# One decoder layer on one Trainium2 core: memory scores kept in PSUM, and transposed outputs taken in one operation

## The chip, the cores and the metric

The kernel runs on one core of one Trainium2 chip. The metric is the device time of one execution in microseconds (us), as the median of several executions. TensorE (PE) multiplies matrices, VectorE (DVE) works elementwise and reduces, ScalarE (ACT) applies functions, GpSimd (POOL) and SyncE (SP) do side work and issue transfers. PSUM is the memory that PE writes to; here it is the tensor `ps`, eight banks of 128 partitions by 512 fp32 words. SBUF is the other on-chip memory.

## The reference

The layer has three groups of heads on one input projection, an output projection, and a mixture of 32 experts (top 4). The change touches only the attention of two of the groups:

```python
s = jnp.einsum('bnqhgd,bnkhd->bnhgqk', qb, kk).astype(jnp.float32) * scale   # sliding window, 6 heads
s = jnp.where(mask[None, :, None, None], s, -jnp.inf)
p = jax.nn.softmax(jnp.concatenate([s, sink], axis=-1), axis=-1)[..., :-1]
...
s = jnp.einsum('bshd,bmhd->bhsm', q, km).astype(jnp.float32) * (HEAD_DIM ** -0.5)   # memory, 4 heads
p = jax.nn.softmax(s, axis=-1)
o = jnp.einsum('bhsm,bmhd->bshd', p.astype(vm.dtype), vm)
```

The sequence has 1024 positions, so 8 blocks of 128; a block of window attention sees 256 keys (its own and the previous 128), and so does a block of memory attention (256 memory tokens). Each group's output is then RMS-normalised with its own gain and goes into the output projection.

## The kernel before

The kernel has one program per engine, and semaphores order them. The stages in time are: norms and the input projection with the recurrent branch; the attention; the output projection with the router; and a loop over the passes of the experts, which takes most of the time.

The attention runs over 16 items, `items`: for each of the 8 blocks first "swa" (sliding window, 6 heads), then "mem" (memory, 4 heads). Item j goes through these steps, each of which is a small function called in an order written out by hand:

- PE `scores(j)` (L1022): one product of 128 queries with 256 keys per head, into banks 0 to 3 of `ps`, which rotate: a swa item takes four banks (its last two heads alone in one each), a mem item two. `scb` counts banks; a bank is written again four banks later, after a wait on `sc_out`.
- DVE `softmax_in(j)`: for swa, three operations (L1521) that scale, add the mask and write to `scores_sb`; for mem, two operations (L1524) that only scale. Then one maximum over all heads (L1527), and a small operation that negates it into `nmx` (L1530, L1535; for swa L1533 too).
- ACT `exps(j, half)` (L684): one exponential per head over 256 keys, `scores_sb` to `scores_sb`, with `nmx` as bias; each also gives the row's sum.
- PE `transpose_probs(j)` (L1038): two heads at a time into bank 4 or 5, from where ACT `take_probs` (L697, bank 4) and DVE `softmax_out` (L1549, bank 5) copy them.
- PE `values(j)` (L1055) into bank 6; DVE `normalise(j)` (L1559) to `o_sb`; ACT `take_o(j)` (L706) squares it for the norm.
- PE `transpose_o(j)` (L1065) into bank 7; DVE `take_y(j)` (L1569): one operation per pair of heads (three for swa, two for mem) that multiplies by a gain column and writes `uT`, counted by `yt_out`.

PE's order for item j is `transpose_probs(j)`, `scores(j + 2)`, `values(j)`, `transpose_o(j - 1)`. DVE's is `normalise(j - 1)`, `softmax_out(j)`, `take_y(j - 2)`, `softmax_in(j + 2)`. ACT's is `exps(j + 1, 0)`, `take_probs(j)`, `exps(j + 1, 1)`, `take_o(j - 1)`, where half 0 holds the first half of the heads. Before this loop DVE does `softmax_in(0)`, `softmax_in(1)` and three products `uT` by gate (L1578), on which POOL's work for the recurrent branch (L494, L496, L498) waits. After it PE sums that branch's squares (L1082) and, once all of `yt_out` has come, starts the output projection `project` (L1102).

Of the kernel before, what the change touches and what calls it, by code (L numbers as in the profile page):

```python
# [22 lines left out]
ALU = mybir.AluOpType  # L23
ACT = mybir.ActivationFunctionType
AX_X = mybir.AxisListType.X

P = 128
# [5 lines left out]
DH = 64  # L33
# [38 lines left out]
def hymba_layer(nc, x, mem, g_mix, w_in, conv_w, conv_b, lru_wa, lru_ba, lru_wx, lru_bx, lru_lambda,  # L72
# [3 lines left out]
    with ExitStack() as ctx:  # L76
# [43 lines left out]
        uT = sb_early("uT", [P, NCT, S])  # L120
# [6 lines left out]
        band = ring[:, 11264:11776].rearrange("p (i k) -> p i k", i=2)  # L127
# [4 lines left out]
        scores_sb = ring[:, 0:4608].rearrange("p (b h k) -> p b h k", b=3, h=NQ)  # L132
# [27 lines left out]
        def col(i, n=1):  # L160
            return vecs[:, i:i + n]
# [6 lines left out]
        nmx, row_sums = ([st[:, base + 8 * i:base + 8 * (i + 1)] for i in range(3)] for base in (0, 24))  # L168
# [25 lines left out]
        with ExitStack() as between:  # L194
# [21 lines left out]
        ps = ctx.enter_context(nc.psum_tensor("ps", [P, 8, HALF], F32))  # L216
# [20 lines left out]
        in_done, in_out = sem("in_done"), sem("in_out")  # L237
# [5 lines left out]
        sc_done, sc_out, nmx_ready, exp_done, sink_in, sink_exp = map(  # L243
            sem, "sc_done sc_out nmx_ready exp_done sink_in sink_exp".split())
        pt_done, pt_act, pt_dve, pv_done, o_ready, o_ss, yt_done, yt_out = map(
            sem, "pt_done pt_act pt_dve pv_done o_ready o_ss yt_done yt_out".split())
# [53 lines left out]

        items = [(kind, b) for b in range(NT) for kind in ("swa", "mem")]

        def heads(kind):
            return NQ if kind == "swa" else NM

        def score_banks(kind):
            return [(0, 2), (1, 3), (4,), (5,)] if kind == "swa" else [(0, 2), (1, 3)]

        scb, hc, ytc = [0], [0], [0]
        for kind, _ in items:  # L310
            scb.append(scb[-1] + len(score_banks(kind)))
            hc.append(hc[-1] + heads(kind))
            ytc.append(ytc[-1] + heads(kind) // 2)
        ptac = [0]
        for kind, _ in items:
            ptac.append(ptac[-1] + (heads(kind) // 2 + 1) // 2)
# [265 lines left out]
        def _(act_e):  # L582
# [25 lines left out]
            for u in range(4):  # L608
                act_e.wait_ge(mkv_done, u + 1)
                dst = km[:, u, :] if u < 2 else vm[:, u - 2, :]  # L610
# [65 lines left out]
            def exps(j, half):  # L676
                kind, b = items[j]
                nh = heads(kind)
                if half == 0:
                    act_e.wait_ge(nmx_ready, j + 1)  # L680
                    if j >= 3:
                        act_e.wait_ge(o_ready, j - 2)
                for h in range(half * (nh // 2), (half + 1) * (nh // 2)):
                    act_e.activation(scores_sb[:, j % 3, h, :], scores_sb[:, j % 3, h, :], ACT.Exp,  # L684
                                     bias=nmx[j % 3][:, h:h + 1],
                                     accum_out=row_sums[j % 3][:, h:h + 1]).then_inc(exp_done, 1)
                if kind == "swa" and half:
                    act_e.wait_ge(sink_in, b + 1)
                    act_e.activation(sinkx[b % 2], sinkx[b % 2], ACT.Exp).then_inc(sink_exp, 1)
# [184 lines left out]
        def _(pe):  # L874
# [15 lines left out]
            for k in range(0, KD, 2):  # L890
                b = bank_of_transposes()
# [109 lines left out]
            def scores(j):  # L1001
                kind, b = items[j]
                lo = P if kind == "swa" and b == 0 else 0
                banks = score_banks(kind)
                for first in range(0, len(banks), 2):
                    for k in (first, first + 1):
                        u = scb[j] + k
                        if u >= 4:
                            pe.wait_ge(sc_out, u - 3)
                        else:  # L1010
                            pe.wait_ge(in_out, 21 + u)
                    for n in range(len(banks[first])):
                        for k in (first, first + 1):
                            h = banks[k][n]
                            r = slice(h % 2 * DH, (h % 2 + 1) * DH)
                            if kind == "swa":
                                qs = uT[r, Q + h // 2, b * P:(b + 1) * P]
                                keys = (uT[r, K, :] if h // 3 == h % 2 else k_other[r, :])[:, (b - 1) * P + lo:(b + 1) * P]
                            else:
                                qs = uT[r, QM + h // 2, b * P:(b + 1) * P]  # L1020
                                keys = km[r, h // 2, :]
                            m = pe.matmul(ps[:, (scb[j] + k) % 4, n * 256 + lo:n * 256 + 256], qs, keys, start=True, stop=True)  # L1022
                            if n == len(banks[k]) - 1:
                                m.then_inc(sc_done, 1)
# [361 lines left out]
        def _(dve):  # L1386
            chain = [0]

            def link(ins):

                chain[0] += 1
                ins.then_inc(dve_step, 1)
                dve.wait_ge(dve_step, chain[0])
# [10 lines left out]
            for n, (a, b) in enumerate(((0, 2), (2, 6), (6, 10))):  # L1404
# [19 lines left out]
                else:  # L1424
                    h = n - 1
                    for k in range(KD):
                        u = 4 + 8 * h + k
# [19 lines left out]
            for c in range(LT):  # L1447
                u, xc = uT[:, LRU + c, :], lru_s[:, 0, :]
# [8 lines left out]
                for back in (1, 2, 3):  # L1457
                    m = dve.scalar_tensor_tensor(out=xc[:, back:S], in0=u[:, 0:S - back], scalar=col(C_CONVW + 3 * (3 - back) + c),
                                                 in1=xc[:, back:S], op0=ALU.mult, op1=ALU.add)
# [4 lines left out]
                t, a, w = lru_s[:, 3, :], lru_s[:, 4, :], lru_s[:, 5, :]  # L1464
# [17 lines left out]
            for u, (h, n) in enumerate(norm_units):  # L1482
                t, w, g = normt[n]
# [3 lines left out]
                                         op0=ALU.mult, op1=ALU.mult).then_inc(normed, 1)  # L1487


            scale = DH ** -0.5  # L1490
            dve.wait_ge(rt_in, 16 * NRT)
            dve.wait_ge(pool_const, NPOOLC)
            link(dve.tensor_scalar(st[:, 88:94], sinkb[:, :], -1.0, None, ALU.mult))
# [1 line left out]
            def softmax_in(j):  # L1495
                kind, b = items[j]
                nh = heads(kind)
                sc = scores_sb[:, j % 3, 0:nh, :]
                banks = score_banks(kind)
                for k, hs in enumerate(banks[:3]):  # L1500
                    n = 2
                    dve.wait_ge(sc_done, scb[j] + (k + 1 if k < 2 else 4))
                    if j == 0 and k == 0:
                        dve.wait_ge(in_done, 24)
                    if j >= 3 and k == 0:
                        dve.wait_ge(pt_done, ytc[j - 2])
                    bank = (scb[j] + k) % 4
                    if k < 2:
                        src = ps[:, bank, :].rearrange("p (h k) -> p h k", h=n)
                        dst = scores_sb[:, j % 3, k:k + 3:2, :]  # L1510
                    else:
                        src = ps[:, bank:bank + 2, 0:256]
                        dst = scores_sb[:, j % 3, 4:6, :]
                    if kind == "swa":
                        if b == 0:

                            dve.tensor_copy(dst[:, :, 0:P], band[:, 1:2, 0:P].to_broadcast([P, n, P]))
                            src, dst, mk = src[:, :, P:2 * P], dst[:, :, P:2 * P], band[:, 1:2, P:2 * P].to_broadcast([P, n, P])
                        else:
                            mk = band[:, 0:1, :].to_broadcast([P, n, 2 * P])  # L1520
                        dve.scalar_tensor_tensor(out=dst, in0=src, scalar=scale, in1=mk,  # L1521
                                                 op0=ALU.mult, op1=ALU.add).then_inc(sc_out, 1 if k < 2 else 2)
                    else:
                        dve.tensor_scalar(dst, src, scale, None, ALU.mult).then_inc(sc_out, 1)  # L1524
                dve.wait_ge(sc_out, scb[j + 1])
                mx = nmx[j % 3][:, 0:nh]
                link(dve.tensor_reduce(mx, sc, AX_X, ALU.max))  # L1527
                if kind == "swa":

                    dve.scalar_tensor_tensor(out=mx, in0=mx, scalar=-1.0, in1=st[:, 88:94],  # L1530
                                             op0=ALU.mult, op1=ALU.min).then_inc(nmx_ready, 1)
                    dve.wait_ge(nmx_ready, j + 1)
                    dve.tensor_tensor(sinkx[b % 2], mx, sinkb[:, :], ALU.add).then_inc(sink_in, 1)  # L1533
                else:
                    dve.tensor_scalar(mx, mx, -1.0, None, ALU.mult).then_inc(nmx_ready, 1)  # L1535

            def softmax_out(j):
                kind, b = items[j]
# [25 lines left out]
            def take_y(j):  # L1564
                kind, b = items[j]
                dve.wait_ge(yt_done, j + 1)
                base, g = (Q, C_GOS) if kind == "swa" else (QM, C_GOM)
                for t in range(heads(kind) // 2):
                    dve.tensor_scalar(uT[:, base + t, b * P:(b + 1) * P], ps[:, 7, t * P:(t + 1) * P], col(g + t), None,  # L1569
                                      ALU.mult).then_inc(yt_out, 1)  # L1570

            softmax_in(0)
            softmax_in(1)
            for c in range(LT):
                u = uT[:, LRU + c, :]
# [334 lines left out]
```

## Time and profile before

| | |
|---|---|
| median of 3 runs | 2197.09 us (2193.68 to 2197.97) |
| the profiled execution's own time | 2191.9 us |
| its span, first to last instruction | 2190.2 us |
| mean granted TensorE clock | 0.987 |
| PE busy | 2109.2 us (96%) |
| DVE busy | 1474.6 us (67%) |
| ACT busy | 1176.3 us (54%) |
| POOL busy | 212.2 us (10%) |

The profile comes from one execution. Its busy shares are averages over all stages; the attention takes the stretch from about 246 to 365 us. In the rows further down, times are us from the start of the span; a row of a timeline gives the start, the duration, the engine, the line, the operation, what it writes and reads and how many instructions are merged in it, and in square brackets how long the engine had been idle and what ended that. A row of a chain gives start, duration and what. The granted clock 1.00 is 2.4 GHz, 0.50 is 1.2 GHz.

### The profile page before, as it was taken

To read this page: it belongs to the slowest core of one execution; us is meant where nothing else is said; L and a number is where in the kernel's file an instruction comes from. 1 tells how busy PE (TensorE), PEld (TensorE's weight loads), DVE (VectorE), ACT (ScalarE), POOL (GpSimd) and SP (SyncE) were. 2 spreads that over 40 slices of the span, in tenths; PEclk is the share of its full clock that TensorE was granted. 3 is DMA by queue.
4 is the path that set the end of the run, shared out by engine and by line. 5 is a ranking of instruction groups with operands and counts; after the bars stand their busy time and mean duration, and the time that the engine had idled before them with its cause. 6 is when DMAs were issued, how large, how long until landed. Compare 5 with 4: busy or idle time off the path is not lost.

```text
span 2190.2 us, 35262 instructions
## 1 busy us (share of the span) xinstructions
PE 2109.2 (96%) x11402; PEld 1665.0 (76%) x11403; DVE 1474.6 (67%) x2299; ACT 1176.3 (54%) x1619; POOL 212.2 (10%) x201
## 2 busy tenths in 40 slices
PE   6999988996999999999999999999999999999997
PEld 4443576554788877977888888887779978888895
DVE  3251485447875688678767676779886567567666
ACT  3241264115665577577555656567775555555555
POOL 2000300003101011011010101010110110101001
PEclk9999999997999999999999999999999999999998
DMA  7000302005986599689877777778996677658556
GB/s 266 1 0 7 148 19 78 39 29 203 341 300 213 185 327 356 229 273 374 298 248 261 248 255 242 255 240 322 369 348 234 211 234 262 201 189 313 186 195 219
DMA packets 203126, 477.36 MB, mean 218 GB/s; under 512 B 14744, under 2 KB 20952, under 8 KB 203025
## 3 DMA queue, kind: packets, MB, share of 16 engines
q1 hardware_dynamic: 185598, 437.69, 54.9%
q0 software_dynamic: 17424, 39.17, 7.4%
q8 instruction: 23, 0.38, 0.1%
q14 instruction: 15, 0.11, 0.0%
q10 hardware_dynamic: 66, 0.02, 0.0%
HBM read 468.99 MB, written 32.11 MB: 229 GB/s over the span
## 4 chain that ended last, share of the span: by engine, by line
PE 81%; DVE 7%; issue 4%; DMA 4%; ACT 2%; ACTq 1%; DVEq 1%; POOLq 0%; POOL 0%; SPq 0%
PE ps L1206 19%; PE ps L1208 18%; PE ps L1207 18%; PE ps L944 8%; PE ps L1102 5%; PE ps L1319 3%; DMA out<-y,idx_cur 3%; DVE w_lo L1739 2%; PE ps L1200 1%; PE ps L1249 1%; DVE st L1527 1%; PE ps L1269 1%; DVE xT L1739 1%; ACT w_hi L811 1%; PE ps L940 1%
## 5 line engine op out<-in xcount | busy, mean ns | idle before, releaser
L811 ACT ACTIVATE w_hi<-ring 128x1024 fp32r<-128x1024 f32 x730 | 781.7, 1121 | 421.1 <-PE ps L1208 372.8
L1739 DVE TENSOR_TENSOR w_lo<-ring,w_hi 128x1024 fp32r<-128x1024 f32 x732 | 862.4, 1220 | 191.2 <-ACT w_hi L811 191.0
L1206 PE MATMUL ps<-xT,w_hi 128*128 128x256 f32 x1248 | 354.2, 284 | 0.0
L1208 PE MATMUL ps<-xT,w_lo 128*128 128x256 f32 x1248 | 353.1, 283 | 0.0
L1207 PE MATMUL ps<-xT,w_hi 128*128 128x256 f32 x1248 | 353.1, 283 | 0.0
L1206 PE MATMUL ps<-w_hi,xT 128*128 128x512 f32 x816 | 323.8, 397 | 12.4 <-issue 6.5
L1207 PE MATMUL ps<-w_lo,xT 128*128 128x512 f32 x816 | 319.8, 392 | 0.0
L1208 PE MATMUL ps<-w_hi,xT 128*128 128x512 f32 x816 | 319.5, 392 | 0.0
L1206 PE MATMUL ps<-w_hi,actT 128*128 128x512 f32 x644 | 262.3, 407 | 0.0
L1208 PE MATMUL ps<-w_hi,actT 128*128 128x512 f32 x644 | 251.5, 391 | 0.0
L1207 PE MATMUL ps<-w_lo,actT 128*128 128x512 f32 x644 | 251.2, 390 | 0.0
L1207 PEld LDWEIGHTS ps<-xT,w_hi 128*128 128x128 f32 x1248 | 239.4, 192 | 0.5
L1206 PEld LDWEIGHTS ps<-xT,w_hi 128*128 128x128 f32 x1248 | 239.4, 192 | 0.5
L1208 PEld LDWEIGHTS ps<-xT,w_lo 128*128 128x128 f32 x1248 | 239.4, 192 | 0.0
L1206 PEld LDWEIGHTS ps<-w_hi,xT 128*128 128x128 f32 x816 | 154.3, 189 | 48.6 <-DVE xT L1739 8.2
L567 POOL DMA_INDIRECT out<-y,idx_cur x45 | 83.3, 1850 | 1094.4 <-ACT y L844 1038.2
L1208 PEld LDWEIGHTS ps<-w_hi,xT 128*128 128x128 f32 x816 | 153.9, 189 | 33.7
L1207 PEld LDWEIGHTS ps<-w_lo,xT 128*128 128x128 f32 x816 | 154.1, 189 | 31.7
L1206 PEld LDWEIGHTS ps<-w_hi,actT 128*128 128x128 f32 x644 | 121.0, 188 | 28.3 <-issue 3.6
L1207 PEld LDWEIGHTS ps<-w_lo,actT 128*128 128x128 f32 x644 | 121.1, 188 | 27.2 <-issue 3.8
L1208 PEld LDWEIGHTS ps<-w_hi,actT 128*128 128x128 f32 x644 | 120.9, 188 | 25.8
L819 ACT ACTIVATE gel<-hm 128x256 f32<-128x256 f32 x180 | 73.4, 414 | 123.1 <-DVE hm L1807 108.4
(284 smaller groups left out, 2324.2 us busy)
## 6 DMA issues: line engine op xcount, KB each, us to landing
ring<-in_w SPq DMA_DIRECT2D x390, 1024.0 KB, 7.3
xh<-in_x SPq DMA_DIRECT2D x4, 2048.0 KB, 16.0
work<-in_w_out SPq DMA_DIRECT2D x1, 4096.0 KB, 12.7
token_rows<-uT POOLq DMA_DIRECT2D x8, 512.0 KB, 2.9
out<-xh SPq DMA_DIRECT2D x8, 512.0 KB, 9.1
work<-in_w_in SPq DMA_DIRECT2D x2, 1536.0 KB, 18.6
uT<-in_w_mem_kv SPq DMA_DIRECT2D x1, 2048.0 KB, 14.2
ring<-in_w_in SPq DMA_DIRECT2D x1, 1536.0 KB, 18.4
```

The costliest lines, as they stand in the source:

```text
L567: po.indirect_dma_start(out=out[0], out_offset=by_index(idx_cur, g), in_=y[:, g, :], in_offset=None, bounds_check=last_row, oob_is_err=Fal ...
L811: act_e.activation(hi, raw, ACT.Copy).then_inc(hi_ready, counted(h, whole))
L819: act_e.activation(gel[:, g, j % 2, :], hm[:, g, j % 2, 0:HALF // 2], ACT.Gelu_apprx_sigmoid).then_inc(gel_ready[g], 1)
L940: m = pe.matmul(ps[:, unit_bank(i), t * P:(t + 1) * P], xnT[:, k, (4 * h + t) * P:(4 * h + t + 1) * P], w[:, k, :], start=k == 0, stop=k = ...
L944: m = pe.matmul(ps[:, unit_bank(i), :], w[:, k, :], xnT[:, k, h * HALF:(h + 1) * HALF], start=k == 0, stop=k == KD - 1)
L1102: m = pe.matmul(ps[:, 2 * g + half, :], uT[:, c, i * P:(i + 1) * P], w_out_sb[:, kk + n, half * HALF:(half + 1) * HALF], start=n == 0, sto ...
L1200: m = pe.transpose(ps[:, bank + k // 4, k % 4 * P:(k % 4 + 1) * P], xg[:, g, k * P:(k + 1) * P], ident[:, :])
L1206: pe.matmul(acc, hi, whi, start=first, stop=False, skip_group_check=shared)
L1207: pe.matmul(acc, hi, wlo, start=False, stop=False, skip_group_check=shared)
L1208: return pe.matmul(acc, lo, whi, start=False, stop=last, skip_group_check=shared)
L1319: m = pe.matmul(acc, actT_f[:, j + k, :], slot(s)[:, 2 * k + b, :], start=first, stop=last)
L1739: return dve.tensor_tensor(lo, x, hi.bitcast(F32), ALU.subtract)
```

## The change

For mem items, DVE no longer copies the scores. The maximum reads them in `ps` (both banks in one operation), the small operation after it multiplies by -scale in place of -1, and ACT's exponentials read `ps` and apply the scale themselves; they write to `scores_sb` as before. The two banks of a mem item are therefore free only when its exponentials are done: PE's `scores` waits for `exp_done` there (bank k of the item: 3 + k of its 4 exponentials) where it waited for `sc_out`. ACT gets one more wait (`pt_done` of the item three back, which used `scores_sb` last). `sc_out` now counts the banks of swa items alone. For all items, `take_y` becomes one operation on two or three tiles at once, with the gain columns broadcast.

```diff
+                        if kind == "mem":
+                            act_e.wait_ge(pt_done, ytc[j - 2])
                 for h in range(half * (nh // 2), (half + 1) * (nh // 2)):
-                    act_e.activation(scores_sb[:, j % 3, h, :], scores_sb[:, j % 3, h, :], ACT.Exp,
-                                     bias=nmx[j % 3][:, h:h + 1],
+                    if kind == "mem":
+                        src = ps[:, (scb[j] + h % 2) % 4, h // 2 * 256:(h // 2 + 1) * 256]
+                    else:
+                        src = scores_sb[:, j % 3, h, :]
+                    act_e.activation(scores_sb[:, j % 3, h, :], src, ACT.Exp,
+                                     bias=nmx[j % 3][:, h:h + 1], scale=scale if kind == "mem" else 1.0,
                                      accum_out=row_sums[j % 3][:, h:h + 1]).then_inc(exp_done, 1)
...
-                        if u >= 4:
-                            pe.wait_ge(sc_out, u - 3)
+                        if u < 4:
+                            pe.wait_ge(in_out, 21 + u)
+                        elif items[sunits[u - 4][0]][0] == "swa":
+                            pe.wait_ge(sc_out, evicted[u - 3])
                         else:
-                            pe.wait_ge(in_out, 21 + u)
+                            pe.wait_ge(exp_done, hc[sunits[u - 4][0]] + 3 + sunits[u - 4][1])
...
+                mx = nmx[j % 3][:, 0:nh]
+                if j >= 3:
+                    dve.wait_ge(pt_done, ytc[j - 2])
+                if kind == "mem":
+                    bank = scb[j] % 4
+                    dve.wait_ge(sc_done, scb[j + 1])
+                    link(dve.tensor_reduce(mx.rearrange("p (n k) -> p k n", k=2),
+                                           ps[:, bank:bank + 2, :].rearrange("p k (n c) -> p k n c", n=2), AX_X, ALU.max))
+                    dve.tensor_scalar(mx, mx, -scale, None, ALU.mult).then_inc(nmx_ready, 1)
+                    return
...
-                    else:
-                        dve.tensor_scalar(dst, src, scale, None, ALU.mult).then_inc(sc_out, 1)
-                dve.wait_ge(sc_out, scb[j + 1])
-                mx = nmx[j % 3][:, 0:nh]
...
-                else:
-                    dve.tensor_scalar(mx, mx, -1.0, None, ALU.mult).then_inc(nmx_ready, 1)
...
-                for t in range(heads(kind) // 2):
-                    dve.tensor_scalar(uT[:, base + t, b * P:(b + 1) * P], ps[:, 7, t * P:(t + 1) * P], col(g + t), None,
-                                      ALU.mult).then_inc(yt_out, 1)
+                nt = heads(kind) // 2
+                dve.tensor_tensor(uT[:, base:base + nt, b * P:(b + 1) * P],
+                                  ps[:, 7, 0:nt * P].rearrange("p (t q) -> p t q", t=nt),
+                                  col(g, nt).rearrange("p (t a) -> p t a", a=1).to_broadcast([P, nt, P]),
+                                  ALU.mult).then_inc(yt_out, nt)
```

## Rows read from the trace of the kernel before

**Rows 1.** The page: busy time of PE, and the granted clock in 40 slices.

```profile
PE 2109.2 (96%) x11402; PEld 1665.0 (76%) x11403; DVE 1474.6 (67%) x2299; ACT 1176.3 (54%) x1619; POOL 212.2 (10%) x201
PEclk9999999997999999999999999999999999999998
```

**Rows 2.** By stretch: length, busy us of PE, PEld, DVE, ACT, POOL, clock, DMA.

```profile
267.00:282.50 15.50, 11.76 (x73) 10.24 (x71) 11.49 (x20) 7.34 (x28) 7.65 (x4) 0.78 0.61 247
282.50:342.70 60.20, 51.61 (x429) 44.55 (x427) 52.29 (x110) 38.48 (x142) 0.00 (x0) 1.00 0.01 1
342.70:364.60 21.90, 17.72 (x148) 15.73 (x147) 14.32 (x35) 11.51 (x39) 0.00 (x0) 0.97 0.00 1
364.60:496.00 131.40, 131.38 (x424) 67.46 (x424) 59.30 (x144) 18.05 (x36) 3.84 (x7) 0.98 0.16 60
```

**Rows 3.** The chain of work over one block: start us, us, what.

```profile
304.89 0.63 PE ps L1038 x4
...
312.52 1.21 DVE ring L1524 x2
313.75 1.23 DVE st L1527
...
316.92 0.63 PE ps L1038 x4
```

**Rows 4.** DVE's timeline in the same block.

```profile
304.52 0.86 DVE L1569 TENSOR_SCALAR uT<-ps,vecs 128x128 f32<-128x128 f32 x3
306.61 1.89 DVE L1521 SCALAR_TENSOR_TENSOR ring<-ps,ring 128x512 f32<-128x512 f32 x3 [1.24 <-PE ps L1022]
```

**Rows 5.** ACT's timeline in the same block.

```profile
303.18 0.51 ACT L684 ACTIVATE ring<-ring,st 128x256 f32<-128x256 f32 x1 [0.54 <-DVE st L1535]
...
306.05 0.50 ACT L684 ACTIVATE ring<-ring,st 128x256 f32<-128x256 f32 x1
...
310.52 0.51 ACT L684 ACTIVATE ring<-ring,st 128x256 f32<-128x256 f32 x1 [2.99 <-DVE st L1530]
...
314.06 0.51 ACT L706 ACTIVATE ring<-ring 128x384 f32<-128x384 f32 x1
...
315.20 0.51 ACT L684 ACTIVATE ring<-ring,st 128x256 f32<-128x256 f32 x1 [0.54 <-DVE st L1535]
```

**Rows 6.** PE's timeline in the same block.

```profile
306.94 2.89 PE L1055 MATMUL ps<-uT,ring 128*128 128x64 f32 x24
...
312.64 2.00 PE L1055 MATMUL ps<-vm,ring 128*128 128x64 f32 x16 [0.64 <-ACT ring L697]
...
314.81 1.04 PE L1038 MATMUL ps<-ident,ring 128*128 128x128 f32 x8
```

**Rows 7.** Groups by line and shape: busy us, mean ns of one, idle before.

```profile
L684 ACT ACTIVATE ring<-ring,st 128x256 f32<-128x256 f32 x80 | 39.6, 497 | 26.2 <-DVE st L1530 22.9 <-DVE st L1535 3.2
...
L1549 DVE COPY ring<-ps 128x512 f32<-128x512 f32 x16 | 11.1, 692 | 9.9 <-PE ps L1038 8.6 <-DVE st L1545 0.5
...
L1559 DVE TENSOR_TENSOR ring<-ps,st 128x256 f32<-128x256 f32 x8 | 3.4, 425 | 3.6 <-PE ps L1055 3.3 <-issue 0.3
...
L844 ACT ACTIVATE y<-ps,gate_cur 128x512 f32<-128x512 f32 x90 | 59.3, 689 | 37.8 <-PE ps L1208 36.3
L832 ACT ACTIVATE actT<-ps 128x256 fp32r<-128x256 f32 x83 | 29.8, 376 | 67.9 <-PE ps L1249 67.9
L826 ACT ACTIVATE actT<-act 128x256 fp32r<-128x256 f32 x78 | 28.0, 413 | 0.0
```

**Rows 8.** Timelines of DVE and POOL at the start of the attention.

```profile
249.90 1.28 DVE L1524 TENSOR_SCALAR ring<-ps 128x512 f32<-128x512 f32 x2
252.55 5.19 DVE L1578 TENSOR_TENSOR uT<-uT 128x1024 f32<-128x1024 f32 x3
...
270.70 1.71 DVE L1530 SCALAR_TENSOR_TENSOR st<-st 128x6 f32<-128x6 f32 x1
...
270.05 4.78 POOL L498 TENSOR_TENSOR work<-work 128x1024 f32<-128x1024 f32 x2
```

More of the change, by code:

```diff
@@ L301, in hymba_layer @@
         items = [(kind, b) for b in range(NT) for kind in ("swa", "mem")]
+        scale = DH ** -0.5
         def heads(kind):
@@ L313, in hymba_layer @@
             ytc.append(ytc[-1] + heads(kind) // 2)
+        sunits = [(j, k) for j, (kind, _) in enumerate(items) for k in range(len(score_banks(kind)))]
+        evicted = [0]
+        for j, k in sunits:
+            evicted.append(evicted[-1] + (items[j][0] == "swa"))
         ptac = [0]
@@ L1487, in _ @@
                                          op0=ALU.mult, op1=ALU.mult).then_inc(normed, 1)
-            scale = DH ** -0.5
             dve.wait_ge(rt_in, 16 * NRT)
@@ L1498, in softmax_in @@
                 sc = scores_sb[:, j % 3, 0:nh, :]
-                banks = score_banks(kind)
-                for k, hs in enumerate(banks[:3]):
+                mx = nmx[j % 3][:, 0:nh]
[8 more added lines that the diff above has]
+                    return
+                for k in range(3):
                     n = 2
@@ L1504, in softmax_in @@
                         dve.wait_ge(in_done, 24)
-                    if j >= 3 and k == 0:
-                        dve.wait_ge(pt_done, ytc[j - 2])
                     bank = (scb[j] + k) % 4
@@ L1513, in softmax_in @@
                         dst = scores_sb[:, j % 3, 4:6, :]
[L1514 to L1518, printed above, removed]
-                        else:
-                            mk = band[:, 0:1, :].to_broadcast([P, n, 2 * P])
-                        dve.scalar_tensor_tensor(out=dst, in0=src, scalar=scale, in1=mk,
-                                                 op0=ALU.mult, op1=ALU.add).then_inc(sc_out, 1 if k < 2 else 2)
-                    else:
-                        dve.tensor_scalar(dst, src, scale, None, ALU.mult).then_inc(sc_out, 1)
-                dve.wait_ge(sc_out, scb[j + 1])
-                mx = nmx[j % 3][:, 0:nh]
+                    if b == 0:
+                        dve.tensor_copy(dst[:, :, 0:P], band[:, 1:2, 0:P].to_broadcast([P, n, P]))
+                        src, dst, mk = src[:, :, P:2 * P], dst[:, :, P:2 * P], band[:, 1:2, P:2 * P].to_broadcast([P, n, P])
+                    else:
+                        mk = band[:, 0:1, :].to_broadcast([P, n, 2 * P])
+                    dve.scalar_tensor_tensor(out=dst, in0=src, scalar=scale, in1=mk,
+                                             op0=ALU.mult, op1=ALU.add).then_inc(sc_out, 1 if k < 2 else 2)
+                dve.wait_ge(sc_out, evicted[scb[j + 1]])
                 link(dve.tensor_reduce(mx, sc, AX_X, ALU.max))
```

## The prediction

> **What bounds the kernel now.** The page comes first: PE is busy for 96% of the span at nearly full clock [rows 1], so DVE and ACT, which this change relieves, bound nothing on average. An average says nothing of one stage, so the second view is the busy time by stretch. In the attention's even part, 282.5 to 342.7 us, DVE is the busiest engine, 52.3 of 60.2 us, with PE at 51.6 and ACT at 38.5 [rows 2]. In the stretch behind it PE is busy for 131.38 of 131.40 us [rows 2]: whatever time the attention hands over earlier, the output projection starts earlier by it, and nothing there absorbs it.
>
> The third view is the chain. It repeats itself exactly: the third transpose of a swa item starts at 304.89 and again at 316.92 [rows 3], a period of 12.03 us for a pair of items. There are five such periods between the starts of the swa evictions at about 282.5 and 342.7, a first one of 15.5 us before them and a tail of 21.9 us behind [rows 2]. Within a period the chain goes from the swa scores over DVE (L1521, L1527, L1530), stays on DVE through the mem item (L1569, L1524, L1527, L1535), then takes ACT (L684, L697), PE (L1038, L1022) and is back at DVE. DVE is idle once in it, 1.24 us ahead of L1521 [rows 4]; ACT is idle for 2.99 us, then, shortly before the mem exponentials, for 0.54 us [rows 5]. That 0.54 is the number on which this case turns: it is all that ACT can move up.
>
> **The change part by part.**
>
> Removed from DVE, in each pair: the two scalings L1524, 1.21 us of the chain [rows 3]. **take_y**: three operations on 128 columns take 0.86 us [rows 4]; one on 384 columns is bounded below by the 128x256 form of L1559, which also has one PSUM operand and a broadcast column, 0.425 us [rows 7], and above by that plus 128 columns at the 0.267 us that 0.692 for 512 and 0.425 for 256 give [rows 7], halved, so 0.56 us. I take 0.56 for three tiles and 0.425 for two. DVE thus gives up about 1.21 + 0.3 + 0.2 = 1.7 us per pair. Were DVE the only limit, five periods would give back 8.5 us. They won't, and the rest says why.
>
> **The maximum from PSUM** isn't in the trace. The nearest rows are the same maximum from SBUF, 1.23 us [rows 3], and two PSUM copies of 512 columns, 2 x 0.692 = 1.38 us [rows 7]. I take 1.23, since the work per column decides in both, and keep 1.38 as its end. Either is hidden: with L1524 gone the mem maximum is out before ACT has finished the swa exponentials.
>
> **An exponential from PSUM** isn't there either. Now one takes 0.497 us [rows 7]. ACT's copy of the very shape 128x256 takes 0.376 from PSUM and 0.413 from SBUF [rows 7], so I take 0.497 - 0.037 = 0.46; the ends are 0.45 and the unchanged 0.50.
>
> **The new loop.** What is late next is ACT. From the start of L1521 at 306.61 to the first swa exponential at 310.52 are 3.91 us [rows 4, 5]; to take_o at 314.06 are 3.54 us more, in which ACT has no gap, and take_o itself is 0.51 [rows 5]. Now ACT waits until 315.20; after the change it goes straight on at 314.57. Two mem exponentials follow, 2 x 0.45 (they overlap their neighbour by some 0.01), then take_probs, 0.57, the interval that ends the chain on ACT. From the end of that copy to PE's next transpose I put 0.15 us, an estimate: the copies' own end to the start of the third transpose in the same block, and from 304.89 to the swa eviction at 306.61 it is 1.72 us [rows 3, 4]. Sum: 3.91 + 3.54 + 0.51 + 0.90 + 0.57 + 0.15 + 1.72 = 11.30 us.
>
> **The added wait.** PE's second pair of swa banks now waits for all four exponentials of the mem item ahead. The last two of them run from 306.05 [rows 5] and would end, with the row sums, at about 307.05, where the products now start at 306.42. Queued behind the waiting product in PE's order are `values` of the swa item (24 products, 2.89 us from 306.94 [rows 6]) and the next item's transposes. The banks come at 307.05 + 0.15 + 0.70 for two heads after a stall = 307.90, and the third L1521 would want them at 307.82: about 0.1 us on the path. `values` then ends at about 310.7, where normalise now starts at 310.63: just covered by the swa maximum. If that cover is gone, each further 0.1 us counts. So the loop is 11.40 us, a gain of 0.63 us per period, and five give **3.15 us**. One more check: the transposes of the next swa item start at 314.81 and their first pair is complete at about 315.41, and ACT will want it at 314.57 + 0.90 = 315.47. PE is 0.06 us away from being the limit: a cheaper exponential than 0.45 would gain nothing.
>
> **The tail.** Behind the last swa maximum the same 0.63 us (315.20 against 314.57 [rows 5]) and twice 0.04 for two exponentials are won, about 0.1 lost at the wait, and the last take_y, on which the projection waits, is 0.425 in place of 0.60: together **0.8 us**.
>
> **The front.** DVE's first mem item loses its scalings too, from 249.90 on, 1.28 us with their gap 1.32 [rows 8]. Nobody waits for its exponentials then, but L1578 starts earlier by that, and POOL's series, started by it, follows. It matters at 270.70: L1530, a matter of 0.17 us, takes 1.71 us there and ends at 272.41, just when the first of the two POOL additions L498 (4.78 us for two from 270.05) ends [rows 8]. Both read SBUF. POOL's addition then ends at about 271.07 and not at 272.39, L1530 is released with it, and the exponentials behind it start 1.3 us earlier. **1.3 us.** The ends: nothing if POOL's second addition gets in first (then a loss of 1.1), 1.5 if no addition is in the way.
>
> The Trainium skill speaks to this place, in SBUF — State Buffer, section Who interferes with whom: a DVE instruction with two SBUF inputs contends with a GpSimd instruction that reads SBUF, and whoever issues first keeps the shared ports. By that rule the stall stays as long as an addition is running when L1530 comes, and shrinks from 1.5 to about 0.2 us, which is the 1.3 above; the trace agrees with its 1.71 us [rows 8].
>
> The rest of the first period is left alone: the clock was 0.78 there [rows 2], and PE sets its length. Nothing else is moved; no DMA and no queue of SP or POOL is touched.
>
> **Sum**: 3.15 + 0.8 + 1.3 = 5.25 us. Against the profiled execution's own 2191.9 that is 2186.6, and its span would be 2185.0. The median of the runs shown is 5.2 us above that execution; against it, 2197.09 - 5.25 = **2191.8 us**.
>
> **The rivals.**
>
> *The held banks come to light.* PE is stalled about 0.8 us per pair at the new wait, and I count 0.1 of it. PE was busy for 51.6 of 60.2 us already [rows 2], and the margins above are 0.06 and 0.1 us. If all of it stood on the path, a period would lose 0.77 - 0.63 = 0.14 us (0.7 in five) and the tail would gain nothing; with the front's 1.3 that leaves a gain of 0.6: 2196.5 us, no difference. For it: PE is in order and `values` stands behind the wait. Against it: DVE spends 3.7 us on the swa scores meanwhile, which don't need `values`.
> The Trainium skill (PSUM — Partial Sum Buffer, Summary: rules for kernel authors) says to evacuate promptly; the change does the opposite, it holds two banks until the exponentials. By that rule this rival is the result; no run here shows it yet.
>
> *The exponential is dearer from PSUM: slower.* Two of the four stand in ACT's part of the loop and two ahead of the new wait, so each 0.1 us more costs 0.4 us per pair, over some seven pairs 2.8 us. The gain is gone at 0.46 + 5.25 / 28 = 0.65 us for one. The only row of ACT that is above it from PSUM, 0.689, is for 512 columns [rows 7]. At twice 0.46 the time would be 2197.1 - 5.25 + 12.9 = 2204.7 us.
>
> *The clock.* In the first period PE is half idle, and the granted clock falls; that period is 15.5 us against 12.03, of which 1.5 are the stall of L1530, so about 1.9 are the clock's. If `values` coming 1.3 us earlier keeps it up, 1.9 us more are won: 2189.9 us. It can also fall elsewhere.
>
> *The change does nothing*: the new forms are split or wait in ways that eat DVE's gain. 2197 us.
>
> **How the numbers follow.** Forecast 0.54, held banks 0.24, clock kept 0.12, dear exponential 0.06, nothing 0.04. The measurement can tell about 0.2%, 4.4 us, from no change. The forecast lies only 0.9 us beyond that; I count 0.42 of its 0.54 as faster and 0.12 as same. Faster: 0.42 + 0.12 = 0.54. Same: 0.12 + 0.24 + 0.03 = 0.39. Slower: 0.06 + 0.01 = 0.07. The forecast's own ends (exponential 0.45 to 0.50, front -1.1 to +1.5) reach from 2191.4 to 2195.4, and the runs before spread over 4.3 us. The range takes in the kept clock below and the held banks above: 2188.5 to 2196.8.
>
> **What would show it.** The period of the chain: 11.4 us (12.0 says nothing was gained, 10.3 that DVE was the only limit). ACT's idle time ahead of L684's mem exponentials gone, that ahead of the swa ones longer than 2.99. L684 in two forms, the PSUM one near 0.46; the PSUM maximum near 1.23. PE waiting for ACT L684 in L1022, 0.7 to 0.8 us, seven or eight times, and L1559 hardly waiting for L1055. L1530's longest near 0.4 in place of 1.71. The projection's first product at about 359.3 where it was 364.6. Wrong would be: a period above 11.7, or a projection that starts earlier while the end doesn't move.

## The result, and the profile after

| | before | after |
|---|---|---|
| median | 2196.09 us (2190.25 to 2198.12, 6 runs) | 2182.65 us (2179.73 to 2187.06, 6 runs) |
| profiled execution's span | 2190.2 us | 2178.0 us |
| mean granted TensorE clock | 0.987 | 0.990 |
| VectorE busy | 1474.6 us | 1459.7 us |

The ratio is 0.9943, with a 95% interval of 0.9931 to 0.9955: about 12.5 us faster (10 to 15). The direction was forecast; the size was not. The sum was 5.25 us, and the time lies below the range. In the two later comparisons the same kernel had ratios of 0.9955 (0.9942 to 0.9969) and 0.9950 (0.9935 to 0.9966).

The first view of after is the groups by line and shape in the attention (busy us, mean ns of one, idle before):

```profile
L696 ACT ACTIVATE ring<-ring,st 128x256 f32<-128x256 f32 x48 | 23.8, 497 | 23.4 <-DVE st L1546 23.4
L696 ACT ACTIVATE ring<-ps,st 128x256 f32<-128x256 f32 x32 | 14.7, 466 | 0.0
L1518 DVE TENSOR_REDUCE st<-ps 128x4 f32<-128x1024 f32 x8 | 9.8, 1222 | 0.6
L1583 DVE TENSOR_TENSOR uT<-ps,vecs 128x384 f32<-128x384 f32 x8 | 4.4, 548 | 0.0
L1583 DVE TENSOR_TENSOR uT<-ps,vecs 128x256 f32<-128x256 f32 x8 | 3.3, 415 | 2.7 <-PE ps L1079 2.7
```

All new prices are as forecast: the exponential from PSUM 0.466 us (0.46), the maximum from PSUM 1.222 (1.23), take_y 0.548 and 0.415 (0.56 and 0.425). The exponentials from PSUM have no idle time before them, where ACT had 0.54 us per block [rows 5].

The second view is the chain over one block (start us, us, what), with lines of waits as short as 0.01 us kept in:

```profile
286.86 1.29 DVE ring L1540 x2
288.15 0.01 DVEq L1524
288.16 0.04 issue
288.20 0.70 DVE ring L1540
...
288.93 1.76 DVE st L1543
...
290.71 0.18 DVE st L1546
...
292.50 0.48 ACT ring L709
292.98 1.48 ACT ring L696 x6
294.45 0.10 ACT st L701
294.55 0.51 ACT ring L718 x2
...
295.31 0.55 ACT ring L696 x2
295.86 0.59 ACT ring L709
...
296.59 0.63 PE ps L1052 x4
297.21 1.11 PE ps L1036 x8
298.33 0.01 DVEq L1524
298.33 0.04 issue
298.38 0.69 DVE ring L1540
```

It goes where the sum went: swa evictions and maximum on DVE, then ACT without a gap through six exponentials, take_o and two mem exponentials, then PE. From 286.86 to 298.38 are 11.52 us; all five periods are so. The forecast was 11.40, and 12.03 before [rows 3].

The third view is the busy time by stretch (length; PE, PEld, DVE, ACT, POOL; clock, DMA), with the attention's stages:

```profile
263.70:275.30 11.60, 9.03 (x71) 7.29 (x71) 8.50 (x16) 7.04 (x27) 6.48 (x3) 1.00 0.81 326
275.30:332.90 57.60, 52.73 (x425) 44.23 (x425) 44.53 (x85) 37.16 (x141) 0.00 (x0) 1.00 0.01 2
332.90:342.40 9.50, 8.86 (x73) 7.74 (x73) 7.75 (x15) 6.22 (x25) 0.00 (x0) 1.00 0.01 3
342.40:345.80 3.40, 2.45 (x20) 2.24 (x21) 1.16 (x2) 2.02 (x8) 0.00 (x0) 1.00 0.00 0
345.80:355.20 9.40, 7.72 (x58) 7.14 (x57) 3.30 (x9) 2.89 (x6) 0.00 (x0) 0.81 0.00 0
355.20:485.00 129.80, 129.80 (x424) 67.13 (x424) 59.21 (x143) 18.04 (x36) 3.84 (x7) 0.99 0.16 61
```

DVE's load in the even part fell from 52.3 us [rows 2] to 44.5 and only 2.5 us came of it. But the first period, 15.5 us at a clock of 0.78 before [rows 2], is 11.6 us here at a clock of 1.00. That is 3.9 us where the sum had 1.3. The projection starts 9.4 us earlier than before (355.2 against 364.6). Of these, 3.9 us are the first period and 2.5 the five periods. The tail gives nothing here: it is 22.2 us against 21.9 before [rows 2], where the sum had 0.8 less, since its last stretch has half clock in it (clock 0.81). The other 3.3 us lie ahead of the first period. The execution before had 6.8 us of half clock near 39 us and this one none, but that can be only a part of them: x_before (below) has none there either, and its first period starts at 266.6, 0.4 us ahead of before. What the two spans share out is thus one draw each; the medians need the experiments.

### The profile page after: what moved, and what is told of

Same layout as the page of the kernel before. It is cut to its first block, busy times and chain, and to the rows that moved or that the text cites. A ratio compares the mean times of both kernels' runs of the same rounds, so it can differ in the third digit from the quotient of the medians.

```text
span 2178.0 us, 35238 instructions
## 1 busy us (share of the span) xinstructions
PE 2103.4 (97%) x11402; PEld 1660.8 (76%) x11403; DVE 1459.7 (67%) x2259; ACT 1174.2 (54%) x1619; POOL 210.8 (10%) x201
## 4 chain that ended last, share of the span: by engine, by line
PE 80%; DVE 6%; issue 4%; DMA 4%; ACT 3%; ACTq 1%; DVEq 1%; POOLq 0%; POOL 0%; SPq 0%
PE ps L1220 19%; PE ps L1222 19%; PE ps L1221 19%; PE ps L956 8%; PE ps L1116 5%; PE ps L1333 3%; DMA out<-y,idx_cur 3%; DVE w_lo L1755 2%; PE ps L1214 1%; ACT ring L696 1%; PE ps L1263 1%; PE ps L1283 1%; DVE xT L1755 1%; ACT w_hi L823 1%; PE ps L952 1%
```

## The experiments

**The kernel before once more, and the change once more.** No edit.

> The kernel before, unchanged, measured against itself. Theory A (stretches of half clock fall by chance from execution to execution): 0 us within 3 us, and the half-clock stretches of its profile lie elsewhere than at 38.8, 274.4 and 363.1 us in part; the 6.8 us stretch at 38.8 us is gone in one or the other. Theory B (they belong to the kernel's own pattern of work): the same three stretches at the same places within 3.4 us, and the first attention period again 15.5 us.

Measured: median 2194.82 us, ratio 1.0003 (0.9989 to 1.0016). Periods 12.03, first period 15.24 us with half clock in it again. But the tail, 21.9 us in the first profile [rows 2], took 27.9 us. The stretches of its tail:

```profile
341.93:351.40 9.47, 8.59 (x73) 7.41 (x70) 9.12 (x19) 5.94 (x24) 0.00 (x0) 1.00 0.01 2
351.40:354.80 3.40, 1.87 (x15) 1.67 (x16) 1.32 (x4) 2.59 (x10) 0.00 (x0) 1.00 0.00 0
354.80:361.60 6.80, 5.91 (x29) 5.54 (x28) 1.85 (x5) 1.18 (x4) 0.00 (x0) 0.50 0.00 0
361.60:369.80 8.20, 7.30 (x35) 6.92 (x35) 2.12 (x8) 1.79 (x3) 0.00 (x0) 0.50 0.00 0
369.80:376.00 6.20, 6.20 (x8) 2.64 (x9) 1.16 (x5) 0.22 (x1) 0.00 (x0) 0.56 0.83 294
```

From 351.4 to 354.8 PE works for 1.87 of 3.40 us; right after it the clock is at 1.2 GHz for 20 us, 5 of them in the projection. The same work in the first profile of the kernel before has the same gaps (1.08 and 0.69 us) and 1.89 of 3.40 us, and keeps its clock for at least 6.8 us more:

```profile
352.20:355.60 3.40, 1.89 (x15) 1.68 (x16) 1.30 (x4) 2.59 (x10) 0.00 (x0) 1.00 0.00 0
355.60:362.40 6.80, 5.91 (x55) 5.70 (x54) 3.03 (x9) 1.86 (x7) 0.00 (x0) 1.00 0.00 0
```

So theory A holds for the start of the kernel and for the tail, theory B for the first period. In 33 more executions of the kernel before on that chip, 21 lie at 2195.6 to 2199.8 us and 12 at 2188.6 to 2193.4, with nothing between. The two kinds aren't that clean everywhere: four of x_before's own ten lie at 2193.7 to 2195.3. But the clock goes with them: the mean granted clock of an execution is 0.987 to 0.989 in the 12 and 0.984 to 0.986 in the 21, which is some 11 us more of half clock (an estimate: twice the difference of the means, 0.0025, times the span). Where it lies only x_before's profile shows.

> The changed kernel again. Theory A: the gain in the median lies nearer to my 5.3 us than the 13.4 us first measured, and the profile has other half-clock stretches than the first one's. Theory B (the gain over 5.3 us comes from half-clock stretches that the change removes): again 11 to 14 us, no half-clock stretch before 340 us, attention's first period 11.5 to 12 us.

Measured: median 2184.24 us against 2196.69 for before, ratio 0.9955 (0.9942 to 0.9969); 8 of 11 executions at 2182.3 to 2185.8 us and 3 at 2188.2 to 2189.4. Both theories were half right. The gain stays at 12.5 us, as theory B had it, but the first period had half clock this time (14.46 us):

```profile
264.00:278.50 14.50, 12.17 (x71) 10.14 (x71) 8.57 (x17) 7.50 (x29) 6.50 (x3) 0.76 0.67 270
```

So half clock comes and goes between executions of one kernel, and the change alters how often.

**One half of the change each.** x_mem keeps the old take_y, x_y has the new take_y alone:

```diff
-                nt = heads(kind) // 2
-                dve.tensor_tensor(uT[:, base:base + nt, b * P:(b + 1) * P],
...
+                for t in range(heads(kind) // 2):
+                    dve.tensor_scalar(uT[:, base + t, b * P:(b + 1) * P], ps[:, 7, t * P:(t + 1) * P], col(g + t), None,
+                                      ALU.mult).then_inc(yt_out, 1)
```

> Only the memory scores stay in PSUM; the transposed outputs are taken in two or three operations as before. My loop has ACT as its limit, so DVE's 0.5 us per pair are worth nothing in it: the period stays 11.5 us, and of the whole gain all but 0.2 us (last take_y) is kept. Rival (DVE is still part of the loop): the period is 11.7 to 12 us and 2 to 4 us of the gain are lost.

Measured: periods 11.52 us, ratio 0.9964 (0.9950 to 0.9978), against 0.9955 for the whole change. DVE isn't in the loop any more: giving back 0.5 us per block costs nothing there. The medians, 2186.83 and 2184.24 us, can't show the 0.2 us that was expected to be lost.

> Only the transposed outputs are taken in one operation; the scores are copied as before. Here take_y of mem items (0.6 to 0.42 us) stands on the chain: the period should be 12.03 - 0.18 = 11.85 us, 0.9 us over five, 0.35 us in the tail: a gain of 1.2 us, with the front unchanged (the first period again 15.5 us). Rival (the half clock of the first period is near a tipping point and any small shift removes it): 3 us or more.

Measured: periods 11.85 us, to the hundredth as expected, first period 15.24; in the ratio nothing, 1.0001 (0.9987 to 1.0015). Its median is 2193.6, but its executions fall into the same two kinds, six at 2190 to 2191 and six at 2196 to 2200, so a gain of 1 us can't be told.

**The front.** f_front keeps the scores in PSUM for the first memory item alone, f_rest for all but the first (both with the new take_y):

```diff
+        def direct(j):
+            return items[j][0] == "mem" and (j == 1)
...
-                    if kind == "mem":
+                    if direct(j):
```

> The change, with the scores kept in PSUM for the first memory item alone (all seven others are copied as before), and take_y in one operation. Theory: this alone lets POOL's additions end 1.3 us earlier, so the stalled L1530 of 1.71 us ends 1.3 us earlier and the first attention period is 13.9 to 14.2 us where it is 15.2 to 15.6, at the same half-clock stretch; the other periods 11.85 us, as with take_y alone. Rival (POOL's series has nothing to do with it, the loop shortens the first period): the first period stays 15.2 us or more.

> The complement: the first memory item is copied as before, all others are kept in PSUM. Theory: POOL's series runs as before, the small operation ahead of the third exponentials is stalled 1.7 us again, first period about 15.2 us with a half-clock stretch in it, then periods of 11.52 us. In the median 1 to 3 us slower than the whole change. Rival: no difference from the whole change, first period at or below 14.5 us.

Measured: in f_rest L1552, which is L1530 of before, is stalled as before, and the first period is 15.3 us. In after, where it is L1546, it takes 0.24 us, and in f_front 0.25. First f_rest, then after, then POOL's work beside it in after:

```profile
267.64 1.71 DVE L1552 SCALAR_TENSOR_TENSOR st<-st 128x6 f32<-128x6 f32 x1
```

```profile
267.60 0.24 DVE L1546 SCALAR_TENSOR_TENSOR st<-st 128x6 f32<-128x6 f32 x1
```

```profile
265.46 4.80 POOL L504 TENSOR_TENSOR work<-work 128x1024 f32<-128x1024 f32 x2
```

The chain scaling, L1578, POOL, L1530 is thereby shown: x_y has the stall, f_front differs from it in the first memory item, and has none. But the first period of f_front was 11.85 us, not 14: it had no half clock. Its later periods were 11.91 us, not 11.85. From the second block on it does what x_y does, but DVE waits for `pt_done` ahead of `sc_done`, as in the whole change. In all six profiles with the 1.71 us stall and no filling there (before, x_before, x_y, f_rest and the later g_before and t_before) the first period is 15.2 to 16.4 us with half clock in it. In the six without the stall and without filling there (after, x_after, x_mem, f_front and the later x_after2 and t_after) it is 11.66, 14.46, 13.15, 11.85, 13.10 and 11.68. What differs for PE is the gap ahead of the second `values`, first before, then after:

```profile
274.56 0.69 PE L1055 MATMUL ps<-vm,ring 128*128 128x64 f32 x2 [3.74 <-ACT ring L697]
```

```profile
269.99 0.77 PE L1069 MATMUL ps<-vm,ring 128*128 128x64 f32 x5 [1.60 <-ACT ring L709]
```

Counted from the first swa eviction, this gap ends 1.26 us earlier, and PE's work ahead of it ends 0.88 us later. It doesn't decide alone: x_after has the same gap, 1.59 us, and had 6.8 us of half clock behind it.

The medians: f_front 2189.24 (ratio 0.9986, 0.9972 to 0.9999), f_rest 2187.55 (0.9982, 0.9968 to 0.9997). They can't be told from each other, and the whole change wasn't run on their chip, so the 1 to 3 us expected between it and f_rest stay open. Two of the nine executions of f_rest took 2196.8 and 2197.4 us at a mean clock of 0.984, though its tail is that of the changed kernel.

**Idle TensorE filled, in both kernels.** The products write a free bank that nobody reads:

```diff
+            def keep_busy(n, bank):
+                for _ in range(n):
+                    pe.matmul(ps[:, bank, 0:256], ident[:, :], km[:, 0, :], start=True, stop=True)
...
+                if j == 1:
+                    keep_busy(12, 7)
+                if j >= 14:
+                    keep_busy(3, 0)
                 values(j)
...
             transpose_o(len(items) - 1)
+            keep_busy(4, 0)
```

> The kernel before with idle TensorE filled by products whose results nobody reads: 12 ahead of the second values, 3 each ahead of the last two values, 4 ahead of the output projection. Theory A (most of the gain above 5.3 us comes from half-clock stretches in the first period and at the projection's start, which the change makes rarer): the first period falls from 15.2 to about 13.7 us, no stretch of half clock of over 7 us around 355 us, the median 3 to 6 us below the kernel before. Rival (the stretches are unrelated to how busy TensorE is there): the same stretches, median within 1 us of the kernel before or above it.

> The changed kernel with the same filling. Theory A: with the clock kept in both, the two differ by my schedule alone: w_before less w_after 5.3 us in the median (4.5 to 7), and w_after is within 2 us of the changed kernel. Rival (the gain is schedule that I overlooked, behind the attention or ahead of it): they still differ by 9 to 13 us.

Measured: w_before 2189.39 us, none of its 11 executions above 2190.1; w_after 2186.61, 2.8 us less where 4.5 to 7 were expected. I had mis-sized the filling: a product of 256 columns takes 0.45 us, so 12 of them 5.4 us. They stood on the path in both kernels, by more where the gap was short (first period 14.2 and 15.2 us). The pair was run again with 5, 1 and 2 products, and in the tail alone.

> The kernel before with fewer filling products, after 12 of them took 5.4 us and stood on the path: 5 ahead of the second values (0.45 us each, 2.2 us in an idle stretch of 3.7), 1 each ahead of the last two values, 2 ahead of the output projection. Theory (in the kernel before, the 3.7 us in which TensorE has no work ahead of the second values bring the half clock every time): first period 13.5 to 14 us (15.2 less the clock's share, with the 1.71 us stall still in it), no half clock in it; median 2187 to 2190. Rival (the first period is long for another reason): 15 us or more.

> The changed kernel with the same filling; the idle stretch there is 1.6 us, so the filling itself puts 0.6 us on the path. Theory: first period 12.3 us, five periods of 11.52, and v_before less v_after is the schedule alone: 1.5 (stall) + 2.6 (five periods) + 0.3 (tail) less 0.6 and less the added wait, so 3 to 5 us. Rival: 8 us or more.

Measured: v_before 2186.76 us, v_after 2183.64: 3.1 us apart, with five executions each and ratios whose intervals overlap (0.9949 to 0.9976 and 0.9935 to 0.9965). The half clock of v_before's first period was to be gone, and part of it stayed. In the profiles the first periods are 14.02 (with 3.4 us of half clock) and 12.15 us, the five periods 60.13 and 57.60, the tails 21.66 and 20.96. The tail and the projection's start of v_before, then of v_after, ran at full clock:

```profile
340.20:361.90 21.70, 19.24 (x157) 16.89 (x155) 14.35 (x35) 11.51 (x39) 0.00 (x0) 1.00 0.00 1
361.90:371.00 9.10, 9.10 (x22) 4.08 (x23) 2.80 (x6) 0.22 (x1) 0.00 (x0) 1.00 0.93 324
```

```profile
335.30:356.20 20.90, 19.35 (x156) 17.16 (x156) 12.12 (x26) 11.07 (x38) 0.00 (x0) 1.00 0.00 1
356.20:366.00 9.80, 9.80 (x24) 4.48 (x24) 2.85 (x7) 0.22 (x1) 0.00 (x0) 1.00 0.89 324
```

The kernel before gains 9.0 us in the median (ratio 0.9963, so 5 to 11 us) from products that compute nothing.

> The kernel before with the filling in the tail and ahead of the projection alone. In the kernel before, two thirds of the executions lie at 2195 to 2200 us and the rest at 2188 to 2193, and the one profile of the upper kind has 20.5 us of half clock from the last items into the projection. Theory (that stretch is the upper kind): the upper kind becomes rare, the median falls to 2190 to 2192, while the first period stays at 15.2 us with its half clock. Rival (the upper kind comes from elsewhere): executions above 2195 stay at half or more.

> The changed kernel with the same filling in the tail. Theory: the executions near 2188 to 2189 (3 of 11 before) become rarer, the median is 2182 to 2184, below t_before by 7 to 9 us, of which 2 to 4 us are the first period's clock. Rival: as slow as or slower than the changed kernel, since two filling products stand on the path, 2185 to 2187.

Measured: t_before 2190.69 us, 5.1 below before, with none of 11 executions above 2194.2; on the same chip 9 of 15 of the kernel before were at 2195 or above. Its first period was 16.4 us, with half clock. t_after 2184.78: 5.9 us below t_before, less than the 7 to 9 expected. t_before leaves the 1.07 us gap ahead of the third transposes of item 14 as it was and narrows the two behind it, from 0.69 and 0.89 us to 0.25 and 0.45, beside the filling ahead of the projection:

```profile
350.75 0.63 PE L1038 MATMUL ps<-ident,ring 128*128 128x128 f32 x4 [1.07 <-ACT ring L697]
352.06 1.66 PE L1055 MATMUL ps<-uT,ring 128*128 128x64 f32 x13 [0.25 <-ACT ring L697]
```

**One gap alone.** In g_before two products stand ahead of the third transpose of item 14 and nowhere else:

```diff
                     pe.wait_ge(exp_done, hc[j] + 2 * k + 2)
+                    if j == 14 and k == 2:
+                        keep_busy(2, 0)
```

> The kernel before with two filling products (0.9 us) in the 1.07 us gap ahead of the last transposes of item 14, and nowhere else. Theory (this gap and the 0.69 us one behind it start the long half-clock stretch, and the change cures it by shortening the first to 0.35 us): no execution, or one in ten, above 2195 us, median 2189 to 2192, as with the whole tail filled (2190.7). Rival (the gaps further on start it): as the kernel before, half or more of the executions above 2195, median 2195 to 2197.

> The changed kernel, unchanged, on the same chip as the two others. 2182.5 to 2184.5 us; g_before less this 6 to 8 us: schedule 3 to 5, the rest the clock of the first period.

> The changed kernel with filling products in gaps only: 3 ahead of the second values (1.34 us in 1.6), 1 each ahead of the last two values. Theory: first period 11.7 us and never a half clock in it, median 1 to 2 us below the changed kernel, 2181 to 2183. Rival: no difference that can be told, since the half clock in the first period was already rare and the one at the projection's start stays.

Measured on one chip: before 2198.23 us with 13 of 17 executions above 2196; g_before 2192.09 with none of 12 above 2195.2; the changed kernel 2186.85; c_after 2184.08. Filling one gap of 1.08 us in a kernel of 2200 us takes 6.1 us off its median (ratio 0.9980, 0.9970 to 0.9991, so 2 to 7 us). The gap in x_before, the same place filled in g_before (L1072 is keep_busy), and what the change makes of it:

```profile
352.24 0.63 PE L1038 MATMUL ps<-ident,ring 128*128 128x128 f32 x4 [1.08 <-ACT ring L697]
```

```profile
350.76 1.03 PE L1072 MATMUL ps<-km,ident 128*128 128x256 f32 x4
```

```profile
342.66 0.63 PE L1052 MATMUL ps<-ident,ring 128*128 128x128 f32 x4 [0.35 <-ACT ring L709]
```

This gap isn't the only one that counts, as the theory had it: t_before left it open, filled what lies behind it, and had no execution above 2195 us either. Either filling is enough.

g_before less the changed kernel is 5.2 us, below the 6 to 8 expected, and the changed kernel was slower than the 2182.5 to 2184.5 expected. c_after, which beats the changed kernel by 2.8 us in the median there, isn't told apart from it: ratios to before 0.9948 (0.9932 to 0.9964) and 0.9950 (0.9935 to 0.9966).

## Why the prediction was wrong

*What bounds the stage, and the new loop*: right. ACT became the limit, DVE's further savings are worth nothing (x_mem), every new operation has its forecast price. The period is 11.52 for 11.40 us. Of the 0.12, some 0.04 are at the third eviction, 0.14 late for the 0.1 put in. Most of the rest is ahead of the first, which starts 1.79 us after the transpose at 296.59 for the 1.72 taken. The chain has an entry "DVEq L1524", the wait for the scores, and 0.04 "issue" there, and the chain before has neither. The edit moved the wait on `pt_done` ahead of this one, and f_front against x_y shows what the order of the two costs, 11.91 us for 11.85. I hadn't priced that. Five periods gave 2.5 us for 3.15.

*The added wait*: right. PE stands 0.6 us at it in each block, and the third eviction behind it is the 0.14 us late:

```profile
287.39 0.45 PE L1036 MATMUL ps<-ring,uT 64*128 64x256 f32 x1 [0.62 <-ACT ring L696]
```

"The held banks come to light" didn't happen. The Trainium skill advises to evacuate promptly (PSUM — Partial Sum Buffer, Summary: rules for kernel authors); holding the banks against this advice cost no more here than that 0.14 us per block. "Dear exponential" and "does nothing" fell with 0.466 us and 11.52 us.

*The front*: the mechanism was right (f_front, f_rest). 1.71 us became 0.24, 1.47 us for 1.3.

*"The rest of the first period is left alone"*: this step failed. I left the half clock there as it was, and had its going as a rival with a chance of 0.12. PE isn't half idle there, as I wrote: it is busy for 11.76 of 15.50 us [rows 2], and most of its idle time is one gap of 3.74 us. More than half of what that gap lost, going to 1.60 us, is the stall I had just removed, and I didn't put the two together. That the gap brings the fall is supported by w_before and v_before, which fill it with the stall still there: none and 3.4 us of half clock, where the unfilled ones have 6.8 or more. Without the stall, three of six profiles have no half clock there, two have 3.4 us of it and one 6.8; the first period is 12.65 us on their mean, not the 14.2 (15.5 less 1.3) of the sum.

*The tail*: this step failed most. Its schedule was right (21.66 us in v_before, 20.96 in v_after, 0.7 for 0.8), its clock wasn't. I read it from one profile, in which it had taken 21.9 us [rows 2]. In x_before it has 20 us of half clock, 5 of them in the projection, and takes 6 us longer; by their times and mean clocks most executions of the kernel before are like this one (21 of the 33), and the median I set my sum against was the median of those. The runs shown, 2197.97, 2197.09 and 2193.68 against the profiled 2191.9, were the hint: I called the 5.2 us between them an offset and carried it over. It was an event at a place where PE has several gaps, and the change shortens the first from 1.07 to 0.35 us, which I could have read off my own schedule. g_before and t_before show that filling idle time there makes the event rare. That the change cures it by this shortening is argued, not shown: before kept its clock behind the same gap, and two executions of f_rest are as slow without it.

So of the 12.5 us: some 5 are the schedule, 4.7 for the 5.25 of the sum (2.5 in the periods, 1.5 in the front, 0.7 in the tail). v_before and v_after, with the tail at full clock in both, give 3.1 in the medians and 5.1 from the first swa eviction to the projection; in the latter are some 1 us of clock in v_before's first period, and my filling, on the path in v_after, hides about 0.5. Some 5 to 6 are the half clock of the tail (t_before, g_before: 5.1 and 6.1 in the medians, each 2 to 7 by its interval). The remaining 1 to 3 are the half clock of the first period: 15.5 us on the mean of six profiles less the stall's 1.47 less 12.65 is 1.4. These parts come from different executions and their sum is no better than 2 us. What stays open is why the changed kernel still has some executions near 2188. The profile of x_after2, 2187.31 us, is nearest to these: against after it starts its first period 3.2 us later, takes 1.4 longer for it, and 2.9 longer behind the projection's start.

## What to carry to other kernels

Read the clock beside the chain, stretch by stretch, and look at TensorE's gaps just before each fall: a stall removed on another engine can shorten such a gap, and what it gives back is then the stall plus the clock. When a profiled execution is faster than the median by more than its spread can explain, the median contains something that this profile doesn't show; profile the unchanged kernel again before summing against it. And when one engine's load is cut, the gain is near the gap of the engine that is next, not near what was cut: here ACT's gap was 0.54 us and the period fell by 0.51, where DVE gave up 1.7.

## What the runs showed of the hardware

Executions of one kernel differ in where they get half clock, but gaps of about 1 us changed the odds: of the kernel before 13 of 17 executions were above 2196 us, with one gap of 1.08 us filled none of 12 (g_before), and with it open and those behind it narrowed none of 11 (t_before). Once at 1.2 GHz, in x_before, TensorE stayed there for 20 us, 5 of them in the projection, although it was busy for 13.2 of the first 15.0 us (5.91 and 7.30 in the rows above). At half clock `values` took 4.30 us in x_before in place of 2.89 [rows 6], so the tail stretched itself. An exponential over 128x256 took 0.466 us from PSUM and 0.497 from SBUF; a maximum over 128x1024 took 1.222 us from two PSUM banks, as from SBUF.
